# Prompt attention with scores, maxima and exponentials two pairs ahead of the transposes, and three probability buffers

## The reference, cut to what matters

```python
def attn_prompt(q, k, v, q_idx, k_idx, w_idx):
    ...
        sc = indexer_scores(qib, wb, k_idx)
        sc = jnp.where((key_pos[None, :] <= pos[:, None])[None], sc, -jnp.inf)
        _, idx = lax.top_k(sc, topk)
        valid = idx <= pos[None, :, None]
        return sparse_attend(qb, _gather_rows(k, idx), _gather_rows(v, idx), valid)
    ...
def sparse_attend(q, k_sel, v_sel, valid):
    ...
    logits = jnp.einsum('btgrd,btkgd->btgrk', qg, k_sel) * (d ** -0.5)
    logits = jnp.where(valid[:, :, None, None, :], logits, -jnp.inf)
    p = jax.nn.softmax(logits, axis=-1)
    o = jnp.einsum('btgrk,btkgd->btgrd', p, v_sel)
```

## Time and profile before

| | us |
|---|---|
| median of 3 runs | 3246.48 (3241.76 to 3248.98) |
| span of the profiled execution, first to last instruction | 3218.5 |
| median less span | 28.0 |
| TensorE busy | 3014.0 (94%) |
| VectorE busy | 1604.0 (50%) |
| ScalarE busy | 1334.5 (41%) |
| GpSimd busy | 262.7 (8%) |

### The profile page before, as it was taken

How to read it: one execution, slowest core, us unless ns; L and a number is a source line. 1 busy time by engine, 2 the same in 40 slices (tenths; PEclk the granted TensorE clock), 3 DMA queues, 4 the chain that set the end, 5 groups by cost and what they waited for, 6 DMA issues and landing times.

```text
span 3218.5 us, 56238 instructions
## 1 busy us (share of the span) xinstructions
PE 3014.0 (94%) x20185; PEld 2635.5 (82%) x20185; DVE 1604.0 (50%) x3493; ACT 1334.5 (41%) x2398; POOL 262.7 (8%) x334
## 2 busy tenths in 40 slices
PE   7999878889999999999989997889899999999998
PEld 5899433558999999999989963346599999999998
DVE  4565699764722322322556567986474222222234
ACT  4433688665522122122443247866564211211234
POOL 1012321011000000000000141100300000000000
PEclk8999989989999999999999998999899999999999
DMA  6622365026311111111432343620642111111124
GB/s 201 163 65 69 108 236 184 2 100 196 99 52 43 48 46 43 48 46 46 116 89 55 69 131 132 209 92 2 230 129 63 45 46 50 46 42 52 46 72 139
DMA packets 356491, 293.60 MB, mean 91 GB/s; under 512 B 85288, under 2 KB 319206, under 8 KB 356024
## 3 DMA queue, kind: packets, MB, share of 16 engines
q1 hardware_dynamic: 325036, 186.21, 19.8%
q0 software_dynamic: 31152, 104.76, 10.5%
q10 hardware_dynamic: 108, 0.11, 0.0%
HBM read 273.33 MB, written 9.78 MB: 88 GB/s over the span
## 4 chain that ended last, share of the span: by engine, by line
PE 64%; DVE 6%; issue 3%; ACT 2%; DMA 1%; POOL 0%; DVEq 0%; ACTq 0%; POOLq 0%; SPq 0%
PE bank L859 44%; PE bank L876 11%; PE bank L843 2%; DVE arena L2635 2%; PE bank L1436 1%; PE bank L1410 1%; DMA arena<-in_cache_v,page_idx 1%; PE bank L917 1%; ACT arena L1902 1%; DVE w_lo L2107 1%; PE bank L1241 0%; PE bank L1370 0%; PE bank L1499 0%; POOL arena L725 0%; ACT w_hi L1629 0%
## 5 line engine op out<-in xcount | busy, mean ns | idle before, releaser
L859 PE MATMUL bank<-h_hi,w_hi 128*128 128x352 f32 x2736 | 891.7, 326 | 11.7 <-DVE arena L2261 7.2
L859 PE MATMUL bank<-h_lo,w_hi 128*128 128x352 f32 x2736 | 880.0, 322 | 0.0
L859 PE MATMUL bank<-h_hi,w_lo 128*128 128x352 f32 x2736 | 879.2, 321 | 0.0
L2107 DVE TENSOR_TENSOR w_lo<-weights,w_hi 128x1024 fp32r<-128x1024 f32 x250 | 306.4, 1225 | 678.0 <-ACT w_hi L1629 671.5
L859 PEld LDWEIGHTS bank<-h_hi,w_hi 128*128 128x128 f32 x2736 | 515.9, 189 | 17.2 <-issue 13.7
L859 PEld LDWEIGHTS bank<-h_lo,w_hi 128*128 128x128 f32 x2736 | 516.5, 189 | 0.3
L859 PEld LDWEIGHTS bank<-h_hi,w_lo 128*128 128x128 f32 x2736 | 515.2, 188 | 0.0
L1629 ACT ACTIVATE w_hi<-weights 128x1024 fp32r<-128x1024 f32 x250 | 264.1, 1056 | 453.3 <-PE bank L859 294.6
L843 PEld LDWEIGHTS bank<-arena 128*128 128x128 f32 (+2 forms) x1717 | 199.3, 148 | 163.3 <-issue 95.3
L843 PE MATMUL bank<-arena 128*128 128x128 f32 (+2 forms) x1717 | 271.1, 290 | 46.1 <-ACT arena L1939 15.8
L876 PE MATMUL bank<-g_hi,w_hi 128*128 128x352 f32 (+2 forms) x768 | 255.7, 333 | 11.1 <-DVE arena L767 5.4
(11 more groups left out here) (396 smaller groups left out, 4369.6 us busy)
## 6 DMA issues: line engine op xcount, KB each, us to landing
arena<-in_w_ada SPq DMA_DIRECT2D x96, 512.0 KB, 4.5
weights<-in_w_down SPq DMA_DIRECT2D x48, 512.0 KB, 3.9
weights<-in_w_gate SPq DMA_DIRECT2D x44, 512.0 KB, 3.8
weights<-in_w_up SPq DMA_DIRECT2D x44, 512.0 KB, 3.8
weights<-in_w_in SPq DMA_DIRECT2D x66, 256.0 KB, 3.8
weights<-in_w_down SPq DMA_DIRECT2D x32, 448.0 KB, 3.6
weights<-in_w_out SPq DMA_DIRECT2D x96, 128.0 KB, 2.9
weights<-in_w_out SPq DMA_DIRECT2D x48, 256.0 KB, 3.1
```

What stands on the lines that cost most here:

```text
L859: mm = pe.matmul(bank[:, 0:TC], wt[:, w], xt[:, x], start=(k + m == 0), stop=(k == n_k - 1 and m == 2))
L2107: dve.tensor_tensor(w_lo[:, w], S(O_W + n % 2 * UNIT, UNIT), w_hi[:, w].bitcast(F32), ALU.subtract).then_inc(unit_lo, 1)
```

## The change

Two pairs run ahead in place of one. TensorE issues qk(0) and qk(1) before its loop and qk(p + 2) in step p; ScalarE runs probs(0) and probs(1) ahead and probs(p + 2) in step p; VectorE runs logits(p + 2) in step p. A third probability buffer takes turns by p % 3; for p > 15 it lies in the unused half of another one. The four pieces of select(1, ...) move ahead of VectorE's loop, two before logits(1) and two behind it, and all later pieces come one step earlier, as does negated. Two work buffers of the selection move to other places in SBUF, and the maxima and their negatives have three slots each.

```diff
-SEL_STEP = {0: ((1, 0), (1, 1)), 1: ((1, 2), (1, 3))}
+SEL_STEP = {}
 for _m in range(2, 7):
     for _k in range(4):
-        SEL_STEP[4 * _m - 6 + _k] = ((_m, _k),)
+        SEL_STEP[4 * _m - 7 + _k] = ((_m, _k),)
...
-        O_EQ, O_CUM, O_GT, O_EQS = (R(5 + n) for n in range(4))
+        O_EQ, O_CUM, O_CUMS, O_GT, O_EQS = H(0), H(1), R(6), R(7), R(8)
...
-        O_PB = [[R(14, 1024 * (2 * t + g)) for g in range(2)] for t in range(2)]
+        O_PB = [[R(14, 1024 * (2 * t + g)) for g in range(2)] for t in range(2)] + [[R(5, 1024 * g) for g in range(2)]]
+
+        def probs_at(p, g):
+
+            return R(14, 1024 * (2 + g) + 512) if p > 15 and p % 3 == 2 else O_PB[p % 3][g]
...
                 qk(0)
+                qk(1)
                 for p in range(32):
-                    if p < 31:
-                        qk(p + 1)
+                    if p < 30:
+                        qk(p + 2)
                     if p % 4 == 1 and p > 4:
                         scales(p // 4 - 1)
                     turns(p)
...
                 probs(0)
+                probs(1)
                 for p in range(32):
-                    if p % 4 == 2 and p < 24:
+                    if p % 4 == 1 and p < 24:
                         negated(p // 4 + 1)
                     turned(p)
-                    if p < 31:
-                        probs(p + 1)
+                    if p < 30:
+                        probs(p + 2)
...
                 logits(0)
+                select(1, 0)
+                select(1, 1)
+                logits(1)
+                select(1, 2)
+                select(1, 3)
                 for p in range(32):
-                    if p < 31:
-                        logits(p + 1)
+                    if p < 30:
+                        logits(p + 2)
```

More of the change, by code:

```diff
@@ L782, in build @@
         O_HIST, O_REJ, O_ABOVE = O_SMALL + 12, R(9), R(9, 128)
-        M_MX, M_NMX, M_SUM, M_RS, M_SMX = (O_SMALL + i for i in (148, 156, 12, 28, 36))
+        M_MX, M_NMX, M_SUM, M_RS, M_SMX = (O_SMALL + i for i in (148, 160, 12, 28, 36))
         ACR, XDT, BTK = ((R(2), R(2, 512)), (R(8, 512), R(8, 768)), (R(10, 256), R(10, 384)))
@@ L1421, in turns @@
                             for k in range(k0, min(k0 + 4, b + 1)):
-                                mm = T(B(bank, [[1, P]], P * (k - k0)), S(O_PB[p % 2][g] + P * k, P))
+                                mm = T(B(bank, [[1, P]], P * (k - k0)), S(probs_at(p, g) + P * k, P))
                             ring.close(mm)
@@ L1916, in negated @@
                         return
-                    step.only(act.activation(neg_s[:, 1024:1024 + NS], S(O_CUM + 1024, NS), ACT.Copy, bias=-BIG, scale=BIG))
-                    step(act.activation(neg_s[:, 0:1024].rearrange("q (r p) -> q r p", r=RUN), S(O_CUM, 1024).rearrange("q (p r) -> q r p", r=RUN),
+                    step.only(act.activation(neg_s[:, 1024:1024 + NS], S(O_CUMS + 1024, NS), ACT.Copy, bias=-BIG, scale=BIG))
+                    step(act.activation(neg_s[:, 0:1024].rearrange("q (r p) -> q r p", r=RUN), S(O_CUMS, 1024).rearrange("q (p r) -> q r p", r=RUN),
                                         ACT.Copy, bias=-BIG, scale=BIG))
@@ L1928, in probs @@
                         act.wait_ge(logits_ready, l * 64 + 2 * p + g + 1)
-                        x = S(O_PB[p % 2][g], P * (b + 1))
-                        act.activation(x, x, ACT.Exp, bias=S(M_NMX + 2 * (p % 2) + g, 1),
+                        x = S(probs_at(p, g), P * (b + 1))
+                        act.activation(x, x, ACT.Exp, bias=S(M_NMX + 2 * (p % 3) + g, 1),
                                        accum_out=S(M_SUM + 8 * (done % 2) + 2 * i + g, 1)).then_inc(probs_ready, 1)
@@ L2736, in select_sample @@
                 def select_sample(k):
-                    eq, cum = S(O_EQS, TOK), S(O_CUM, TOK)
+                    eq, cum = S(O_EQS, TOK), S(O_CUMS, TOK)
                     if k == 0:
@@ L2775, in logits @@
                             settle(dve)
-                            Dr.done(dve.tensor_tensor_reduce(out=S(O_PB[p % 2][g] + c0, w), in0=bank[:, 0:w], in1=mask, scale=HD ** -0.5, scalar=-3e38,
-                                                             op0=ALU.add, op1=ALU.max, accum_out=S(M_MX + 4 * (p % 2) + 2 * g + c, 1)), wait=(c0 + w == full))
+                            Dr.done(dve.tensor_tensor_reduce(out=S(probs_at(p, g) + c0, w), in0=bank[:, 0:w], in1=mask, scale=HD ** -0.5, scalar=-3e38,
+                                                             op0=ALU.add, op1=ALU.max, accum_out=S(M_MX + 4 * (p % 3) + 2 * g + c, 1)), wait=(c0 + w == full))
                     k = (full + 511) // 512
                     for g in range(2):
-                        dve.tensor_reduce(S(M_NMX + 2 * (p % 2) + g, 1), S(M_MX + 4 * (p % 2) + 2 * g, k), AX.X, ALU.max, negate=True).then_inc(logits_ready, 1)
+                        dve.tensor_reduce(S(M_NMX + 2 * (p % 3) + g, 1), S(M_MX + 4 * (p % 3) + 2 * g, k), AX.X, ALU.max, negate=True).then_inc(logits_ready, 1)
                 def turned(p):
```

## The result

| | us |
|---|---|
| kernel before, median of 20 runs beside the change | 3247.62 (3239.42 to 3254.87) |
| changed kernel, median of 20 runs | 3254.80 (3248.29 to 3262.75) |
| ratio | 1.0027, 95% interval 1.0019 to 1.0035 |
| span of the changed kernel's profiled execution | 3253.3 |
| forecast | 3245.5, range 3237.0 to 3253.0 |

The change costs 0.27%, some 7 us: slower by more than the 0.2% that I had put in the middle of my cases.

What follows compares the result with a forecast made beforehand. TensorE was the bound on the average, with stage time counting in full through the gathers behind it. -8.54 - 2.8 + 7.48 + 2.83 + 2.0 = 1.0 us gained: span 3217.5, with 28.0 carried over 3245.5 us, range 3237 to 3253.

Steps and rivals of the forecast that it cites:

- The median is 28.0 above it, and I carry that over.: Whole kernel: the runs' median, 3246.48 us, lies 28.0 above the profiled span of 3218.5; added to the forecast span.
- Tiles 8 to 15 go out ahead of these, after logits(31), which the change brings forward too.: Around the stage's end: these gathers go out from 711.63 us, ahead of tile 16, and earlier with the change.
- The fill: Start of the stage: one turns and pv lost while VectorE is late, 4.27 us a layer, 8.54 in all.
- The clock at the start: Start of the stage: new idle time may drop TensorE's clock; half a 2.83 us spell, 1.4 a layer, 2.8 lost.
- the slow rival: Steps 0 to 4 of each layer: TensorE at 1.2 GHz behind 588 us, two spells a layer; 3254.0 us, chance 0.15.
- The late waits: Late in the stage: TensorE's waits of 0.76, 1.73 and 1.25 us go, 3.74 a layer, 7.48 in all.
- the spell of layer 0: Layer 0, steps 23 to 31: half clock behind the 1.73 us gap costs 2.83 us, taken as gone.
- the clock at the end: End of the stage, L1448: runs at 2.4 GHz once the 1.25 us gap closes, about 1.0 us less, 2.0 for two layers.
- The sum: Whole kernel: losses and gains add to 1.0 us gained, span 3217.5, time 3245.5; no change that can be measured.
- The third-bank waits: Steps of blocks 7 to 4: TensorE waits 0.25 to 0.58 us for ScalarE's copy, some fifteen a layer; unchanged.
- The end keeps its full clock: Faster rival, first work behind the stage at 2.4 GHz: about 3.8 us less a layer, 3237.9 us, chance 0.19.
- Stage time counts in full: Gathers behind the stage, 29.7 us, start as much earlier as the stage ends earlier, once in each layer.

Runs made afterwards that it cites:

- second profile of before: The kernel before, unchanged, profiled and timed again: 3244.87 us, ratio 0.9997, span 3252.1.
- both edits: Gathers of tiles 0 to 6 spread over steps 25 to 31, tiles 8 to 15 behind the last heads: before 3235.70 us, changed 3235.72.
- lead from step 16: Changed kernel with the second step of lead only from step 16 on: 3242.93 us, ratio 0.9986; with both edits 3225.76 us, ratio 0.9946.
- lead at the start: Changed kernel with two steps of lead only in steps 0 to 15, one step from 16 on: 3252.78 us, ratio 1.0021.

## Why the prediction was wrong, point by point

**"The median is 28.0 above it, and I carry that over."** This step hid the one that failed. I took the distance as overhead; 2.2 us of it are. The rest is time that ordinary executions lose and the profiled one didn't: in the second profile of before the last weigh lies 11.9 and 9.6 us later after the first qk than in the first, 21.5 us in all (10.9 more lie ahead of the first stage, in an execution slow for its kernel). A trace that runs 0.8% under the median of its own kernel lacks something that the others have. Carrying the 28.0 over is harmless to the difference of the kernels only if both lose alike, and they don't.

**"Tiles 8 to 15 go out ahead of these, after logits(31), which the change brings forward too."** This is the step that failed. The fact was right, and I priced it at nothing ("no wait is new"). The term that is missing is what the row of issues costs TensorE's signals: 5.5 us in layer 0 and 6.0 in layer 1 between last scales and last weigh, with the scales' signal 7.5 and 7.0 us late. From the first profile it couldn't be sized, since its scales' signal was 0.04 us late; but the question what a moved step collides with was there, and I asked it only of data, not of the issuing engine.

**The fill, 4.27 us a layer.** Right. turns(2) at 25.49 and 25.62 us (forecast 25.7), the gap 3.37 (forecast about 3.1). The kernels with both edits, changed against lead from step 16, differ by 4.4 us a layer at the last pv.

**The clock at the start, 1.4 us a layer.** Too large. The 4.4 us hold it too, which leaves little over 0.1 us a layer. The extra spell at 1.2 GHz lies 8.4 to 15.3 us behind the first qk (layer 0, both edits), mostly in time that TensorE waits anyway; the slow rival's spell behind 588 us didn't come.

**The late waits, 3.74 us a layer, "the spell of layer 0" and "the clock at the end", 1.0.** Between the kernels with both edits, before against lead from step 16, the end of the stage gains 4.5 us to the last pv and 0.6 more to the last scales, 5.1 a layer; forecast were 3.74 + 1.4 (half the spell) + 1.0 = 6.1. By waits alone it is less: from step 16 to the last pv TensorE waits 4.4 us in the one (1.73, 0.76, 0.67, 0.58, 0.34, 0.33) and 2.2 us in the other, where the new waits of 1.05 and 0.53 us stand. I had named neither: scales(4) waits for VectorE's reciprocals, so VectorE was late in the middle, not only at the very end. The spell in layer 0 didn't occur in either kernel with both edits. Another part is the last 2 us before the last pv, at half clock in the one kernel and full in the other; some 1 us of the 4.5 I can't put on rows. So the sum of the end came out right to 1 us a layer while its parts did not.

**The sum, 1.0 us gained.** To the last scales, with both edits, 0.8 us a layer, 1.6 in all; the times are 3235.70 and 3235.72. The balance of the order was right, in part by luck: the start was put 1.3 us a layer too dear (4.27 + 1.4 against 4.4) and the end 1.0 too high (6.1 against 5.1), and these cancel. It wasn't the whole change.

**The third-bank waits** are as before. **"The end keeps its full clock"**, the faster rival, half came: the first transpose takes 1.06 us in place of 1.94 and the first weigh comes 1.2 and 2.1 us earlier after the last scales; the last weigh is only 0.7 and 0.5 us earlier, no more than the last scales were, since it hangs on transfers by then. **Stage time counts in full** fell with it: in the changed kernel even a gain of 2.0 us at the last scales (layer 0) ended as a loss of 3.5 at the last weigh.

**What stays open.** In all kernels that start the row of tiles 8 to 15 at logits(31) behind an unchanged row of tiles 0 to 6, it starts 3.7 to 4.2 us ahead of the end of the last scales (layer 0), so my wording that the lead starts the row too early relative to them doesn't hold. Yet the signal was late by 0.04, 2.51 and 1.45 us where the stage ended with one step of lead (before twice, lead at the start; layer 1: 0.04, 0.90 and 0.88), and by 7.4 to 7.7 us where it ended with two (layer 1: 6.8 to 7.7). In the two ordinary executions with one step it came while the row was still being issued, 4.9 to 6.4 us after its start; in those with two it came only 1.9 to 2.7 us after the last issue. The former had their scales at half clock (1.97 to 1.98 us for 16 matmuls), the latter at full (1.09). Whether the clock, or what TensorE sent just before, makes the difference wasn't tried, so why the change meets the row worse than the kernel before stays open. Nor is it known why one execution of before showed no late signal at all.

## What to carry to other kernels

Compare the span of a profile with the time of its kernel's runs before building on it; 25 us missing here were another condition, not overhead. When a change moves the release of GpSimd's indexed gathers, look at which signals of TensorE fall into the row. Spreading tiles 0 to 6 over steps gained some 9 us here; moving the row of tiles 8 to 15 alone gained nothing, since it met the weighs, and paid only together with the other edit. A longer lead costs its fill where another engine is late at the start; letting it grow where the waits are gained another 10 us (3235.72 to 3225.76).

## What the runs showed of the hardware

- Where a row of eight indexed gathers, one issued every 1.24 us, ran beside the last scales, TensorE's signal came late by 0.9 to 7.7 us, and by 9.5 and 10.3 in a row of ten. Where the lead was two steps it came 1.9 to 3.1 us after the last issue. One execution, the first profile of before, had the same rows and no late signal. It happened at 48 GB/s (0.18 of the DMA engines) and didn't happen with plain transfers of the same bytes at 351 GB/s.
- In such a row TensorE also issued slowly: 64 matmuls in 9.4 us in place of 3.64 (changed kernel, row of tiles 8 to 15 moved later, layer 0).
- A gather took GpSimd 0.94 + 0.30 us to issue, a plain transfer 0.54. With an eighth of the bytes the gather still took 0.94.
